# Splitting fp32 weights for the tensor engine: a mixture-of-experts stage with one half of w1 in plain fp32, w3 with stacked row halves, and all low halves made by one engine

## What is computed

```python
# first block
mod = c @ w_ada + b_ada                      # shift, scale, gate
h = rmsnorm(x) * (1 + scale) + shift
proj = h @ w_in                              # q k v z_ret u_val u_gate z_conv g_a g_b
ret = head_groupnorm(retention(q, k, v))     # 4 heads
y_a = (ret * silu(z_ret)) @ w_ret_out
a = causal_depthwise_conv(u_val * sigmoid(u_gate))
a = silu(layernorm(a))
y_b = (a * silu(z_conv)) @ w_conv_out
# second block: window attention, spatial gating, cross-attention, then 32 experts, top 2
for each block of slots with expert e:
    hid = silu(xblk @ w1[e]) * (xblk @ w3[e])    # 1024 -> 512
    y[tokens] += slot_w * (hid @ w2[e])          # 512 -> 1024
```

## Time and profile before

| | us |
|---|---|
| median of 3 runs | 1807.93 |
| lowest and highest | 1804.19, 1810.4 |
| the profiled execution, its own time | 1806.99 |
| its span, first to last instruction | 1805.2 |
| busy PE, DVE, ACT, POOL | 1683.2, 1129.6, 913.4, 860.5 |
| data moved by DMA | 340.94 MB |

### The profile page before, as it was taken

One profiled execution on the slowest core, in us unless ns is written; L12 is line 12 of the kernel. 1 busy time (PEld: TensorE's weight loads), 2 busy tenths in 40 slices (PEclk: granted clock), 3 DMA queues, 4 the chain that ended last, 5 costly groups with the idle time before them and its releaser, 6 DMA issues.

```text
span 1805.2 us, 23103 instructions
## 1 busy us (share of the span) xinstructions
PE 1683.2 (93%) x7444; PEld 1237.4 (69%) x7444; DVE 1129.6 (63%) x1455; ACT 913.4 (51%) x1228; POOL 860.5 (48%) x451
## 2 busy tenths in 40 slices
PE   1899999989999999899998999968999999999996
PEld 1788888767778788678856886655566665666664
DVE  4667765481422457434475444156999899998996
ACT  3545443443222332243442235335888888888885
POOL 0488886324334344324202331203766767667774
PEclk9899999989999999999988999988999999999998
DMA  8344444222221163522211520056999999999994
GB/s 300 86 120 114 112 148 172 70 105 90 80 99 49 46 222 140 189 90 90 93 47 47 161 93 21 32 229 219 362 378 377 373 375 379 376 371 385 388 374 153
DMA packets 135407, 340.94 MB, mean 189 GB/s; under 512 B 14582, under 2 KB 66046, under 8 KB 110507
## 3 DMA queue, kind: packets, MB, share of 16 engines
q1 hardware_dynamic: 127938, 320.71, 49.0%
q0 software_dynamic: 5200, 8.41, 2.1%
q10 hardware_dynamic: 2200, 10.92, 1.6%
HBM read 329.78 MB, written 18.87 MB: 193 GB/s over the span
## 4 chain that ended last, share of the span: by engine, by line
PE 67%; POOL 9%; issue 8%; DVE 7%; ACT 4%; DMA 2%; DVEq 1%; POOLq 0%; ACTq 0%; SPq 0%
PE ps L718 16%; PE ps L719 16%; PE ps L720 16%; POOL parts L2393 7%; PE ps L690 5%; PE ps L1079 3%; PE ps L930 3%; PE ps L1080 2%; POOL out L2416 2%; PE ps L700 2%; ACT arena L1511 2%; DMA ring<-in_w_ada 2%; DVE arena L2284 1%; PE ps L1041 1%; PE ps L958 1%
## 5 line engine op out<-in xcount | busy, mean ns | idle before, releaser
L2360 POOL TENSOR_TENSOR parts<-ring,parts 128x1024 fp32r<-128x1024 f32 x158 | 391.4, 2484 | 697.3 <-ACT parts L1129 641.8
L718 PE MATMUL ps<-parts,act_parts 128*128 128x512 f32 (+2 forms) x1152 | 454.8, 395 | 13.4 <-DVEq L1768 5.6
L720 PE MATMUL ps<-parts,act_parts 128*128 128x512 f32 (+2 forms) x1152 | 450.1, 391 | 0.0
L719 PE MATMUL ps<-parts,act_parts 128*128 128x512 f32 (+2 forms) x1152 | 449.6, 390 | 0.0
L1481 ACT CAST parts<-ring 128x1024 fp32r<-128x1024 f32 x384 | 396.4, 1048 | 93.6 <-PE ps L720 70.2
L2244 DVE TENSOR_TENSOR parts<-ring,parts 128x1024 fp32r<-128x1024 f32 x289 | 394.2, 1414 | 25.5 <-ACT parts L1481 18.6
L1129 ACT CAST parts<-ring 128x1024 fp32r<-128x1024 f32 x158 | 163.7, 1048 | 349.1 <-PE ps L720 293.6
L2393 POOL TENSOR_TENSOR parts<-ring,parts 128x1024 fp32r<-128x1024 f32 x95 | 262.5, 2763 | 144.3 <-ACT parts L1481 143.6
L718 PEld LDWEIGHTS ps<-parts,act_parts 128*128 128x128 f32 (+1 forms) x1152 | 190.6, 165 | 105.1 <-POOL parts L2393 18.5
L718 PE MATMUL ps<-act_parts,parts 128*128 128x512 f32 x640 | 252.0, 394 | 4.9 <-DVEq L1671 4.9
L719 PE MATMUL ps<-act_parts,parts 128*128 128x512 f32 x640 | 249.7, 390 | 0.0
(11 more groups left out here) (265 smaller groups left out, 1791.8 us busy)
## 6 DMA issues: line engine op xcount, KB each, us to landing
ring<-in_w SPq DMA_DIRECT2D x192, 1024.0 KB, 7.4
ring<-in_w_in SPq DMA_DIRECT2D x30, 1024.0 KB, 7.2
ring<-in_w_in SPq DMA_DIRECT2D x34, 512.0 KB, 5.2
ring<-in_w_ada SPq DMA_DIRECT2D x12, 1024.0 KB, 12.5
ring<-in_w_ret_out SPq DMA_DIRECT2D x8, 1024.0 KB, 6.3
ring<-in_w_out SPq DMA_DIRECT2D x8, 1024.0 KB, 8.2
ring<-in_w_in SPq DMA_DIRECT2D x16, 256.0 KB, 4.1
gates_dram<-arena ACTq DMA_DIRECT2D x8, 512.0 KB, 5.6
```

Of the source, the lines that this page charges most:

```text
L718: pe.matmul(o, lhs[1], rhs[0], start=start, stop=False)
L719: pe.matmul(o, lhs[0], rhs[1], start=False, stop=False)
L720: return pe.matmul(o, lhs[0], rhs[0], start=False, stop=stop)
L2360: pool.tensor_tensor(parts[:, g % 4, 1, :], ring[:, st.place(j), k * 1024:(k + 1) * 1024], parts[:, g % 4, 0, :].bitcast(F32), ALU.subtrac ...
```

## The change

*Experts.* The first half of w1 (pieces 0 and 1) is no longer split. TensorE multiplies it as it lies in the ring, in fp32, by fp32 rows `xg_rows` that ScalarE copies; a new semaphore `w1_half_used` frees the half. The other ten pieces go through five buffers (`piece_parts`, the fifth in the rows' memory) instead of four. w3 uses the form that w2 had: both row halves as 128 stationary columns, two matmuls instead of three; ScalarE copies the lower product (`up_low`), VectorE adds. The gate is one Silu by ScalarE. VectorE makes all ten low halves, GpSimd none.

```diff
-                    for c in range(2):
-                        if before is not None:
-                            sp.wait_ge(piece_split[4 * j + 2 * n + c], before)
+                    if before is not None:
+                        if j == n == 0:
+                            sp.wait_ge(w1_half_used, before)
+                        else:
+                            for c in range(2):
+                                sp.wait_ge(piece_split[4 * j + 2 * n + c], before)
...
+                o = bank(stage, 1, i)
+                pe.wait_ge(half_landed[0], (b + 1) * 16)
+                pe.wait_ge(xg_rows_ready, b + 1)
+                for t in range(KT // 2):
+                    mm = pe.matmul(o[0:SLOTS, :], xg_rows[:, t, :], ring[:, 0, t * FF:(t + 1) * FF], start=t == 0, stop=False)
+                mm.then_inc(w1_half_used, 1)
...
+                for n in range(2, 8):
+                    if n == 4:
+                        o = bank(stage, 2, i)
+                    pe.wait_ge(piece_split[n], b + 1)
...
                         else:
-                            mm.then_inc(moe_used[n], 1)
+                            rows = xgT[:, t].rearrange("p h s -> p (h s)")
+                            pe.matmul(o, rows, w[:, 0, half], start=t == 0, stop=False)
+                            mm = pe.matmul(o, rows, w[:, 1, half], start=False, stop=t == KT - 1)
...
+            def gate(stage, i=0):
+                drained(stage, 1, act.activation(t_h[0:SLOTS, :], full(stage, 1, i)[0:SLOTS, :], ACT.Silu))
...
+            def low_up(stage, i=0):
+                act.copy(up_low[0:SLOTS, :], full(stage, 2, i)[SLOTS:2 * SLOTS, :]).then_inc(up_low_ready, 1)
...
             with dve.Fori(0, dve.snap(steps - 1)) as r:
                 moe.enter(r, 4)
-                for n in (0, 1, 2):
-                    low(n, r * 12 + (20 + n))
-                low_hidden("moe", r + 1, r)
+                for n in (2, 3, 4, 5):
+                    low(n, r * 10 + (14 + n))
                 add_rows(r)
-                for n in (4, 5, 6):
-                    low(n, r * 12 + (20 + n))
-                gate("moe", r + 2, r + 1)
-                for n in (8, 9, 10):
-                    low(n, r * 12 + (20 + n))
+                low_hidden("moe", r + 1, r)
+                for n in (6, 7, 8, 9, 10, 11):
+                    low(n, r * 10 + (14 + n))
                 hidden("moe", r + 2, r + 1)
```

```diff
-    ("hT", KT, 1), ("columns", 1, 1), ("mod", (1,), 1), ...
+    ("columns", 1, 1), ("hT", KT, 1), ("mod", (1,), 1), ...
...
+            sp.dma_start(x0, x_v).then_inc(x_in, 16)
+
             def ada(stage, j, g):
                 chunk(stage, j, lambda r: pair(r, w_ada[:, :, g * 512:(g + 1) * 512]))
 
+            sp.wait_ge(const_in, 16)
             ada("ada", 0, 0)
-            sp.wait_ge(const_in, 16)
-            sp.dma_start(x0, x_v).then_inc(x_in, 16)
+            sp.wait_ge(x_in, 16)
+            ada("ada", 1, 1)
             sp.wait_ge(weights_landed[0], 32)
-            ada("ada", 1, 1)
-            sp.wait_ge(x_in, 16)
             ada("ada", 2, 2)
+            sp.wait_ge(weights_landed[1], 32)
             ada("ada", 3, 3)
...
+                n = 2 if g < 3 else 1
                 for c in range(4):
-                    mm = product(o[:, 4 * g + c:4 * g + c + 1], [ada_sum[:, 2 * g + q, c * P:(c + 1) * P] for q in range(2)],
-                                 [cst("ones")[:, 0:1]] * 2)
+                    mm = product(o[:, 4 * g + c:4 * g + c + 1], [ada_sum[:, 2 * g + q, c * P:(c + 1) * P] for q in range(n)],
+                                 [cst("ones")[:, 0:1]] * n)
```

```diff
-                    own(act.activation(convT[:, t, :], convT[:, t, :], ACT.Identity, bias=bias, scale=g))
-                    own.wait()
-                    act.activation(ln_s[:, t % 2, :], convT[:, t, :], ACT.Sigmoid).then_inc(ln_s_ready, 1)
+                    act.activation(convT[:, t, :], convT[:, t, :], ACT.Silu, bias=bias, scale=g).then_inc(ln_s_ready, 1)
...
-                    act.activation(sig_r[:, m % 2, :], o, ACT.Sigmoid).then_inc(sig_r_ready, 1)
+                    own(act.activation(z_tok[:, m, :], full(f"hz{h}", m), ACT.Silu))
+                    own.wait()
+                    drained(f"hz{h}", m, act.nop())
+                    act.nop().then_inc(z_ready, 1)
```

More of the change, by code:

```diff
@@ L1641, in weigh_rows @@
                 dve.nop().then_inc(weights_used[s], 1)
+                if stage == "ada" and j == 3:
+                    own(dve.tensor_tensor(dst[:, 0, :], dst[:, 0, :], dst[:, 1, :], ALU.add))
+                    own.wait()
                 dve.nop().then_inc(ada_ready, 1)
@@ L2344, in _ @@
             for n in (8, 9, 10, 11):
-                low(n, steps * 12 + n)
+                low(n, steps * 10 + (n - 2))
             add_rows(steps)
```

197 lines of the change are left out of this document (86 added, 111 removed).

## The result

| | before | after |
|---|---|---|
| median, us | 1806.06 (4 runs) | 1766.90 (4 runs) |
| the profiled execution, its span | 1805.2 | 1768.4 |
| ratio, 95% interval | | 0.977 [0.9756, 0.9784] |

The account below looks back on a forecast made before the run. Split loop and TensorE were taken to set today's 17.37 us expert round, with DMA engines nearly full and bounding next at 17.1. Gains of 8.6 + 8.0 + 13.7 = 30.3 us gave 1777 us, range 1752 to 1798.

Parts of the forecast that it names:

- Opening, -8.6 forecast: Opening: x and w_ada's first block load earlier, fewer column products; modulation starts at about 50.8 us instead of 59.4.
- earlier than TensorE gets there: Opening: VectorE has block 3 weighed and its halves summed by 46.2 us, before TensorE, whose products run to 50.1.
- a fixed 15.5 us to x's landing: Opening: x, issued at about 1.7 us, lands after the same 15.5 us as before, at 17 to 18.
- Head 0, -8.0 forecast: Head 0: one-step Silu gates shorten TensorE's 6.8 us wait for VectorE and avoid 2.2 us lost at half clock.
- The 1.0 us of wait that was left in the sum: Head 0: TensorE's wait for VectorE's last gated product shrinks from 6.8 us to 1.0.
- Experts, -13.7 forecast: Experts: 4.9 us from the first four rounds, 7.3 from 27 later rounds, 1.5 at the end.
- 27 rounds gain 0.27 each: Experts: DMA engines hold all rounds after the first four at 17.1 us instead of 17.37, 7.3 us together.
- 1.9 for the stall and 1.0 for a round: Experts' beginning: the first round loses a stall worth 1.9 us; each other round of the first four gains 1.0.
- The DMA engines go faster when asked: Rival, experts: VectorE bounds rounds at 16.3 us, gaining 35.5 instead of 13.7, total 1756 us; chance 0.2.
- The expert rounds gain nothing: Rival, experts: DMA engines are full; only opening, head 0 and the end gain, 18 us, total 1790; chance 0.18.
- The opening does not move: Rival, opening: another landing holds it, total 1786 us; chance 0.05.
- The half clock in the experts: Rival, experts: TensorE falls to half clock before the hidden rows are turned; 1836 us if every round; chance 0.07.

Follow-up runs that it names:

- the later versions: Changed kernel with conv_w's 31 rows loaded by two DMAs, 1760.39 us; that also without SyncE's waits, 1760.79; or with the last w2 in ring place 0, 1760.82.
- the other run: The changed kernel, nothing altered, run and traced again on the chip of three further versions: 1766.24 us, 0.9794 of the kernel before.
- with less compute: Changed kernel with all DMAs, without products with w3's and w2's low halves, those halves made for half their columns: 1760.03 us, 0.9762 of before.
- the fewer-bytes kernel: Changed kernel loading only 256 of 2048 columns of w2's second half for every expert but the first: 1745.16 us, 0.9673 of before.

## Why the prediction was right, and where it was off

The gain was forecast at 30 us and came out at 39. The opening and head 0 came by the steps that were forecast, up to one in the opening that failed; in the experts the bound was the right one and the way that it acts on the rounds was not.

*Opening, -8.6 forecast, -9.4 measured.* Every landmark came within 1 to 2 us: x at 18.5 (17 to 18), block 0 at 24.6 (23.5), block 3 at 41.3 (40.5), modulation at 50.1 (50.8). The step that failed is the last: "earlier than TensorE gets there". The column products were costed at the 12.19 / 64 us a pass of the earlier trace rows, and passed in 5.62 / 48 = 0.12, so TensorE waited for block 3's sum, and the landing bound the opening. The 0.19 us was the price at clock 0.57, which the prediction did not look up; at 0.95 it is not paid. The sum ended at 50.8 where the landings gave 50.1, and that they lie so close is luck. What was taken as a fixed 15.5 us to x's landing was a lagging engine, and worth another 5.5 us.

*Head 0, -8.0 forecast, -8.5 measured* (17.8 us ahead at 742 us, less the opening). The 1.0 us of wait that was left in the sum is not there, and the clock stayed up. On the way to the experts 2.7 us are lost again, at 1085 and 1116 us, where the profiled run shows the clock at half for a while; the run of the same kernel beside the later versions has no such loss and is 21.1 us ahead there. That is the scatter between runs, not the change.

*Experts, -13.7 forecast, -21.7 measured* (-19.7 in the other run). The compute loop was forecast at 16.4 us and is 16.14, and from 1500 to 1700 us the engines moved the 383 GB/s that the 17.1 us of the forecast stand for. The step that failed is "27 rounds gain 0.27 each": the DMA bound was taken as one number for all of them, with slack for the first four. It is not one number. In the first nine rounds behind the first scatter the engines moved 399 GB/s, and with less compute such a round took 16.14 us, no longer than the loop, so these gained 1.1 us each in place of 0.27. In the last 13 the bound is 17.4 us, and they gained nothing. The early rounds carry fewer bytes of rows, and the queue had room as well: a half lands 10.4 us after its issue from 1260 to 1385 and 13.1 from 1500 to 1700, where it was 7.5 before, and while this grew the loop ran ahead of the engines. The 29 rounds gained 503.0 - 488.9 = 14.1 us instead of 9.3. The beginning, to the first scatter, gained 4.7 us (3.3 in the other run), which the sum had at 1.9 for the stall and 1.0 for a round; over this stretch the mean granted clock was 0.91 (0.88 in the other run) instead of 0.86. The end gained 2.9 instead of 1.5. The mean over the 29 rounds, 16.86 us, is near the forecast's 17.1, with a spread that the forecast did not have.

*The rivals.* Two of them were each right for a part of the rounds. "The DMA engines go faster when asked" holds for the early ones, 399 GB/s instead of 371 at the same share, and it has the time within 11 us; it does not hold beyond that, since with less compute they gave 403 early and 383 late. "The expert rounds gain nothing" is what the last 13 did. "The opening does not move" did not come. The half clock in the experts was refuted by the window above: TensorE is idle (400 - 383.1) / 24 = 0.7 us a round and the clock reads 1.00; with less compute it is idle 2.4 us a round, and the clock reads 0.91, so the mechanism exists where the waits are longer. SyncE's new wait for w1's first half was costed at nothing, rightly for the compute loop: the fewer-bytes kernel has it too, and holds 16.14 us in every round. Whether it costs anything in the later rounds, where the share is 0.98, no run tells.

What the prediction did not see at all is the strongest effect of the case: what GpSimd's low halves cost VectorE depends on what VectorE does beside them. It priced them by the mean (1.36 against 1.17), which is right for removing all three; for w3's form alone the same pricing promised 9 to 18 us and the run lost 102.

## What to carry to other kernels

Take the parts of a change apart in their dependence, too: here w3's stacked form, which reads as TensorE's saving, costs 102 us while GpSimd still makes low halves, and taking these from GpSimd leans on the fp32 half, which costs TensorE time. When a loop gets faster than a DMA queue that reads as full, don't take one number for the bound: a share of 1.00 stood here for 371 and for 399 GB/s, and the bytes of a round were not the same in all of them. Before the price of an instruction is read from a row, look up the clock of that row. And before the time to landing of a large load is taken as given, look beside it for a small DMA whose packets go one behind another.

## What the runs showed of the hardware that was not expected

- VectorE's instructions with both operands in SBUF wait while GpSimd runs an elementwise instruction on SBUF (0.74 us becomes 2.05; three low halves of 3.50 became 6.78 in one round and 5.61 in another beside one of GpSimd's, in the changed kernel with GpSimd's low); those with an operand in PSUM do not (0.67 us beside it).
- A MB of weights costs the 16 engines 2.48 us in the changed kernel, early and late, a MB of gathered and added rows 4.2 to 4.4 us. The first of these is no constant: from 1260 to 1660 us it is 2.60 in the kernel before, 2.69 with all 12 low halves by VectorE, 2.74 with w3 stacked alone. In these three a half lands after 7.4, 6.6 and 5.8 us, where the changed kernel has 11.7, and their share reads 1.00, 0.98 and 0.88. The cause was not looked for.
- TensorE's one-column passes cost 0.19 us at a granted clock of 0.57, 0.12 at 0.95 and 0.23 at 0.50.
- One DMA of 31 rows of 4 KB delays the landing of a 2 MB load beside it by 4.6 us (18.49 to 13.89); as 16 and 15 rows it does not. The page that the expectation quotes is DMA: Bandwidth & Descriptors in the Trainium skill; its rule on the number of engines agrees with this run.
